# A weight ring in SBUF begins 40 bytes past a multiple of 64 instead of 24

## The reference

```
x = x + 0.5 * (silu(h @ w1_gate) * (h @ w1_up)) @ w1_down      h = RMSNorm(x)
z = RMSNorm(x) @ w_in                                          2824 columns
att = sliding-window attention, 8 query heads, 2 kv heads, learned sinks
lstm = chunkwise mLSTM, 4 heads of 128
x = x + concat(att, RMSNorm(sigmoid(o) * lstm)) @ w_out
x = x + 0.5 * (silu(h @ w2_gate) * (h @ w2_up)) @ w2_down      h = RMSNorm(x)
y = RMSNorm(x)
```

## Time and profile before

| what | value |
|---|---|
| median of three runs | 1943.49 us (1942.76 to 1945.61) |
| the profiled execution | 1942.99 us |
| its span, first to last instruction | 1941.4 us |
| TensorE busy, weight loads busy | 1923.0 us (99%), 1879.8 us (97%) |
| VectorE, ScalarE, POOL busy | 1282.4, 783.1, 1050.7 us |
| granted TensorE clock | 0.998 of full speed |
| matmuls | 14627, of which 7488 take their weights from `WR` |

### The profile page before, as it was taken

The page is one execution under the profiler, slowest core; times in us unless marked ns, Lnnn a source line. Parts: engine busy times, 40 slices in busy tenths (PEclk is TensorE's granted clock), DMA queues, the critical chain, the costliest instruction groups (busy, mean ns, idle before and its releaser), DMA issues.

```text
span 1941.4 us, 39225 instructions
## 1 busy us (share of the span) xinstructions
PE 1923.0 (99%) x14627; PEld 1879.8 (97%) x14627; DVE 1282.4 (66%) x1882; ACT 783.1 (40%) x1595; POOL 1050.7 (54%) x958
## 2 busy tenths in 40 slices
PE   8999999999999999999999999999999999999998
PEld 7999999999999999999998999999999999999997
DVE  7766776666567778864445664866767667656774
ACT  6433333333443345733334642443333333344343
POOL 3277776775777641321222442237767776686770
PEclk9999999999999999999999999999999999999999
DMA  8135455444986530342332834214454344498552
GB/s 272 46 116 181 135 167 175 133 132 157 312 316 186 173 102 15 115 120 89 101 104 62 208 94 124 79 56 145 152 181 142 133 155 164 150 367 272 165 157 104
DMA packets 226846, 293.88 MB, mean 151 GB/s; under 512 B 16616, under 2 KB 158472, under 8 KB 226736
## 3 DMA queue, kind: packets, MB, share of 16 engines
q1 hardware_dynamic: 219040, 272.76, 43.8%
q0 software_dynamic: 7696, 19.63, 3.2%
HBM read 198.07 MB, written 94.21 MB: 151 GB/s over the span
## 4 chain that ended last, share of the span: by engine, by line
PE 92%; POOL 2%; DVE 2%; DMA 1%; ACT 1%; issue 1%; SPq 0%; ACTq 0%; DVEq 0%; POOLq 0%
PE bank L292 28%; PE bank L293 28%; PE bank L294 28%; PE bank L2585 1%; PE bank L2604 1%; PE bank L2595 1%; POOL HA L1388 1%; DMA WRAW<-in_w_down 1%; DMA XIN<-in_x_prompt 1%; PE bank L2516 0%; PE bank L1335 0%; PE bank L1334 0%; PE bank L1333 0%; PE bank L1329 0%; PE bank L2696 0%
## 5 line engine op out<-in xcount | busy, mean ns | idle before, releaser
L292 PE MATMUL bank<-HA,HW 128*128 128x272 f32 x1120 | 322.7, 288 | 0.4 <-DVE HW L1382 0.4
L294 PE MATMUL bank<-HA,HW 128*128 128x272 f32 x1120 | 321.7, 287 | 0.0
L293 PE MATMUL bank<-HA,HW 128*128 128x272 f32 x1120 | 321.4, 287 | 0.0
L1382 DVE SCALAR_TENSOR_TENSOR HW<-WRAW,HW 128x512 fp32r<-128x512 f32 x140 | 224.2, 1639 | 104.4 <-ACT HW L1377 103.9
L1388 POOL TENSOR_TENSOR HA<-ARAW,HA 128x544 fp32r<-128x544 f32 x140 | 220.7, 1593 | 102.8 <-ACT HA L1376 102.7
L292 PE MATMUL bank<-HL,WGH 128*128 128x368 f32 (+2 forms) x784 | 255.7, 326 | 0.0
L293 PE MATMUL bank<-HH,WGH 128*128 128x368 f32 (+2 forms) x784 | 246.3, 314 | 0.5 <-issue 0.5
L294 PE MATMUL bank<-HH,WGL 128*128 128x368 f32 (+2 forms) x784 | 246.5, 314 | 0.0
L293 PE MATMUL bank<-FC,WR 128*128 128x272 f32 x768 | 222.2, 289 | 0.0
L292 PE MATMUL bank<-FC,WR 128*128 128x272 f32 x768 | 220.5, 287 | 1.1 <-DVE WR L966 0.4
L294 PE MATMUL bank<-FC,WR 128*128 128x272 f32 x768 | 220.2, 287 | 0.0
(11 more groups left out here) (384 smaller groups left out, 5668.5 us busy)
## 6 DMA issues: line engine op xcount, KB each, us to landing
asp<-SA SPq DMA_DIRECT2D x44, 544.0 KB, 3.4
RAWG<-in_w_gate SPq DMA_DIRECT2D x22, 1024.0 KB, 6.4
RAWU<-in_w_up SPq DMA_DIRECT2D x22, 1024.0 KB, 6.4
tsp<-TT SPq DMA_DIRECT2D x40, 544.0 KB, 6.5
ARAW<-tsp SPq DMA_DIRECT2D x80, 272.0 KB, 3.4
WS<-in_w_down SPq DMA_DIRECT2D x20, 1024.0 KB, 8.8
wsp<-WS SPq DMA_DIRECT2D x20, 1024.0 KB, 8.5
WRAW<-wsp SPq DMA_DIRECT2D x80, 256.0 KB, 4.1
```

Source lines behind the costliest of these rows:

```text
L292: nc.tensor.matmul(bank[:, 0:w], w_hi, one, start=first, stop=False)
L293: nc.tensor.matmul(bank[:, 0:w], w_hi, two, start=False, stop=False)
L294: return nc.tensor.matmul(bank[:, 0:w], w_lo, rhs_hi, start=False, stop=last)
L1382: nc.vector.scalar_tensor_tensor(out=HW[f][h][:, 1], in0=WRAW[r][:, :], scalar=0.5, in1=HW[f][h][:, 0].bitcast(F32), op0=ALU.mult, op1=ALU ...
```

## The change

The lead in front of the region wg becomes 40 bytes, and the rest behind it 24 in place of 8. Before, lead and rest were 32 bytes together, now they are 64. So:

- `WR`, and what else is placed at `rWG` (`SS`, the raw down weights `RAWD`, the weight sums `WS0` and `WS1`, the last gain `GF`), begins 40 bytes past a multiple of 64, 16 bytes later than before.
- `WGH` and `WGL`, placed at `rWG - WEIGHTS`, stay where they were.
- raw, d, t and c begin 32 bytes later: at a multiple of 64, where they were 32 past one. They hold the raw weights, `PV`, `SA`, `WB`, the attention's and mLSTM's tiles and the constants.
- x, hh, hl and a, and with them the moving operands of the FFN, stay. `HW` keeps its 24 bytes under a name of its own.

```diff
-WEIGHTS = 24
+WEIGHTS, SLOT_WEIGHTS = 40, 24
@@
         region("lead", WEIGHTS)
         rWG = region("wg", 2 * 4 * 4096)
-        region("rest", 32 - WEIGHTS)
+        region("rest", 64 - WEIGHTS)
@@
-        HW = [[place(f"HW{f}{h}", [P, 2, 512], F32R, slot_at[f][h] + 4352 + WEIGHTS) for h in range(SLOTS)] for f in range(2)]
+        HW = [[place(f"HW{f}{h}", [P, 2, 512], F32R, slot_at[f][h] + 4352 + SLOT_WEIGHTS) for h in range(SLOTS)] for f in range(2)]
```

## The result

The changed kernel took 1949.08 us in the median of 7 runs (1947.51 to 1952.94), against 1943.66 us (1942.76 to 1945.61, 7 runs) before. The ratio is 1.0026, with a 95% interval of 1.0017 to 1.0035: slower by 5.4 us, a small change that is clear of the noise. The profiled execution took 1949.08 us, 6.1 us more than that of before.

What follows compares the result with a forecast made beforehand. TensorE, a pure chain of matmul starts in the gate-and-up stages, was taken as the bound. 1942.99 + 0.9 - 0.3 = 1943.6, or 1944.1 against the median; the forecast said 1944.2 us, range 1934.5 to 1956.0.

Steps and rivals of the forecast that it cites:

- the lever: Gate-and-up stages of both FFNs: one nanosecond of pitch on all 7488 matmuls is 7.49 us, sign open.
- The likeliest case: Ring stages keep nearly their pitch, 124.6 ns, for 1944.2 us; with the case of no effect, chance 0.38.
- The pitch stays in this narrow band: Ring stages: weights 8 past a multiple of 16, at 40 as at 24, hold 124.5 to 124.7 ns.
- the prediction's own signs: Wrong if the ring's two frame halves show pitches apart, or the whole kernel changes by over 4 us.
- The term (124.6 - 124.48) x 7488 = +0.9 us: Ring stages of both FFNs: pitch rises from 124.48 to 124.6 ns on 7488 matmuls, +0.9 us.
- w_out's places: w_out, 24 matmuls each, read as frame quarters 2, 3 and 0: 126.7, 123.3 and 125.4 ns, differing by row starts.
- The prediction's sign for the opposite: FFN down's 119.7 us or w_out's 3.04, 2.96, 3.01 us moving would mean pitch hangs on something other than addresses.
- The rival on the slow side: Ring stages slow to as much as 126.7 ns, +16.6 us, or 125.1 ns, +4.9 us; chance 0.36.
- Half of it, if only one frame half does: Ring stages: only one frame half falls into the slow pattern, +8.3 us, 1952; part of the slow side's 0.36.
- The rival that weights' starts do nothing: Ring stages: pitch depends only on where rows begin, 1943.5 us; chance 0.38 together with the prediction's own case.
- The cover and the other parts: Writers and transfers stay hidden behind ring matmuls; attention, mLSTM and transposes bounded by 1.5 us either side, taken as 0.
- The term of -0.3 us for `WB`: Last FFN pair: weights move to a multiple of 64, 1 to 2 ns on 144 matmuls, up to 0.3 us back.

Runs made afterwards that it cites:

- e6: Changed kernel with the ring's weights starting 8 bytes past a multiple of 64 in place of 40: 1948.43 us, one run.
- e4: Changed kernel with the ring's weights starting 56 bytes past a multiple of 64 in place of 40: 1955.61 us, one run.
- e7: Changed kernel with the ring's weights starting 32 bytes past a multiple of 64 in place of 40: 1945.50 us, one run.
- e1: Changed kernel with the ring back at 24 bytes, the regions behind it left where the change put them: 1944.84 us, ratio 1.0001 to the kernel before.
- e2: Changed kernel with 16 bytes of padding ahead of all regions and the ring 24 bytes from the rows' alignment: 1946.24 us, ratio 1.0011 to the kernel before.
- e9: Changed kernel with one extra fp32 matmul of 125, 126 or 127 columns at three places in each FFN's ring stages: 1953.63 us.

## Why the prediction was right, and where it was wrong

**What bounds, and the lever.** Right. The stages are a pure chain of starts; 5.0 of the 6.1 us appear in the two windows. A pitch of 124.83 ns over one stage and 125.67 over the other makes (0.35 x 3744) + (1.17 x 3744) = 5.7 us by the prediction's own count; from first to last ring matmul it was 1.0 + 4.3 = 5.3, mainly because the first FFN's third block, which holds the pause, took 10.73 us in place of 11.03 and so gave 0.3 back.

**The likeliest case.** Wrong. It forecast 0.7 us more than the median it knew, and 5.4 were measured. "The pitch stays in this narrow band", 124.5 to 124.7 ns, was taken from the evenness of ring and FFN down and explained by starts of 8 past a multiple of 16. The evenness was real, but it was that of one distance, 24, which all those stages share. By the prediction's own signs it was wrong too: the frame halves have pitches apart, and the whole changed by over 4 us. The starts of 8 and 56 (e6, e4) break the explanation, 32 (e7) breaks it from the other side. The term (124.6 - 124.48) x 7488 = +0.9 us should have read about +0.35 ns for the first FFN and +1.17 for the second.

**w_out's places.** Misread, in the prediction and in the captions of the earlier trace rows. `out_step` cuts the first 32 chains of w_out to 12 matmuls, one for each frame quarter in turn, so 24 matmuls there span two quarters. VectorE, which adds each finished chain to the residual, shows the step: its adds (L2393) lie 1.52 us apart there, 12 matmuls. So a new chain starts between the two rows, at 1166.06, and one between those of the earlier trace rows, at 1170.54:

```profile
1164.74 0.44 DVE L2393 TENSOR_TENSOR X<-X,bank 128x272 f32<-128x272 f32 x1 [1.08 <-PE bank L294]
...
1166.06 0.29 PE L292 MATMUL bank<-HL,WGH 128*128 128x272 f32 x1
...
1166.26 0.44 DVE L2393 TENSOR_TENSOR X<-X,bank 128x272 f32<-128x272 f32 x1 [1.08 <-PE bank L294]
...
1170.54 0.29 PE L292 MATMUL bank<-HL,WGH 128*128 128x272 f32 x1
```

Counted so, hold quarters 2 and 3, quarters 1 and 2, and the earlier trace rows quarter 3. Quarter 2 takes 1.52 us for 12 matmuls in the first (1164.54 to 1166.06) and 1.48 in the second (1170.54 to 1172.02), and the moving rows are the very same, for both chains take the second half of the contraction. What differs is the slot of the weights: `WGH` has four, 4096 bytes apart, one for each 128 output columns. In all twelve profiles that left w_in's and w_out's addresses alone, slot 3 runs at about 123.3 ns, slot 2 at about 126.6, slot 1 mostly at 126.7, and slot 0 mostly at 125.3, whatever the quarter and in both halves of w_out, which put different weights there. So these rows did not show that "what differs is where the rows begin against the weights". That addresses count at all was right, and e1 shows it. The prediction's sign for the opposite, these stretches taking another time at kept addresses, came true once, with 3.04 us for the 3.01 of the earlier trace rows: addresses set the pitch only together with the pattern that the chain is in.

**The rival on the slow side.** It was the closest. The mean of w_out's three places, 125.1 ns, gave 1948.4 us; the measured mean of the two stages is 125.25. Its reason, that 24 stands below the middle of what this shape shows and a new place is more likely worse, agrees with the table: of five other starts four are slower and none faster. "Half of it, if only one frame half does" has the form of the first FFN, where half 0 alone slowed, by 0.7 ns; in the second FFN both halves did, to 125.2 and 126.1 ns, and neither reached 126.7.

**The rival that weights' starts do nothing.** Refuted by e1: 24 against 40 with all else equal, 10.46 against 10.52 and 10.59 us a block. The prediction's step from the rule in the Trainium skill, that TensorE never waits for another engine's port, to "no start address would change the pitch" fails by the same runs; who waits for whom they do not show. That 24 and 40 touch the same number of 16-byte lines, and so should be alike, fails too.

**The cover and the other parts.** Right in the main. Writers kept their durations, and e1 puts the regions behind the ring at 1.6 us less to 2.1 us more, no narrower than the prediction's 1.5 us either side. The term of -0.3 us for `WB` came from the lengths of single matmuls and not from a pitch; its 144 matmuls gave back 0.16 us (26.65 to 26.49 from first to last). 108 more in the second FFN's last pair, which it left out, gave back 0.26 (32.59 to 32.33). e1 reads the same on both.

**What I did not foresee** is that one set of addresses has two pitches. The prediction's signs to look for said "two frame halves with pitches apart"; two FFNs apart was not among them.

**The range** held the time, 1934.5 to 1956.0, which is wide enough for the slow side and the fast side alike; that is in part luck, since the likeliest case was off by 4.9 us. Its upper end leaned on w_out's 126.7 ns, a pitch that was measured but not for the reason given. The ring at 56 reached 1955.61 us. Its lower end is 1943.5 - 8.8, which is 1934.7 and not 1934.5; nothing hangs on it.

**Open.** Why a distance is good or bad is not shown: six starts give no rule that I can state. Nor is what picks the pattern at an entry, nor why w_out's slots differ. What rows and weights moved together cost (e2) has no cause here. No run moved the rows alone, and none told TensorE's two reads of the memory apart from the traffic of the other engines on it; that blocks repeat to 2 ns speaks against the latter, no more.

## What to carry to other kernels

Where TensorE is a chain without waits, the start of the stationary operand within a partition is a parameter worth up to 1.8 ns of 124.5 a matmul at 272 columns in this kernel's ring, and it has to be measured for each stage: evenness at one distance says nothing on another. Read it from the distance between block starts in a single profile, which repeats to a few nanoseconds in 10 us, rather than from the time of the kernel. And take more than one profile, since one layout can run at two pitches. Before a pitch is put down to an operand, count the matmuls of a chain in the code: 24 matmuls held two quarters here, and the cause that was read into them was wrong.

## What the runs showed of the hardware that was not expected

- Two persistent patterns at the same addresses: blocks of 84 matmuls at 10.46 or 10.59 us, each held over many blocks, one turned into the other by one small extra matmul at 1407.19 us in e9.
- Weight starts at 8, 24, 32, 40, 48 and 56 bytes past a multiple of 64 gave 125.3, 124.5, 124.5, 125.7, 125.0 and 126.3 ns a matmul. A shift by 32 bytes is not neutral, 24 against 56.
- In w_out the pitch goes with the slot of the weights, 4096 bytes apart: 126.7 ns in slot 2 and 123.3 in slot 3, for the same frame quarter. With weights and rows both moved by 16 bytes (e2), the slot 3 stretch at the place of the earlier trace rows went to 126.7 ns.
- After a disturbance the chain returns to its pattern: the block that follows the nudge takes 10.60 us in place of 10.52, the next blocks their usual times.
